# A two-layer, two-block network on one core: a new order for the first stage (early products of ones, bias rows, memory root, index heads)

## The chip, the cores and the metric

The kernel runs on one core of a Trainium2 chip. The metric is the device time of one execution in microseconds (us), as the median of several executions. A core has TensorE (PE, with its weight loads as PEld), VectorE (DVE), ScalarE (ACT), GpSimd (POOL) and SyncE (SP), which here only issues DMAs. Engines run their own instructions in order and wait for each other by semaphores.

## What is computed

Four layers on x of 256 rows by 1024 columns: two layers of a first network (each a mixer and a convolutional feed-forward part), then two of a second one, whose mixers also attend to a memory of 256 rows. The change lies in the first mixer, and it is enough to see this much of the reference:

```
h = x @ w_in                      # q_a, c_kv, q_idx, k_idx, w_idx, q_b, k_b, v_b, f_in
log_f = log_sigmoid(f_in + b_f); cum_f = cumsum(log_f)
idx = einsum('bthd,bsd->bths', q_idx, k_idx)             # 8 index heads
score = einsum('bth,bths->bts', w_idx, relu(idx)); sel = top_k(score, 64)
la = q_lat . c_kv[sel] + rel_bias[t5_bucket(q_pos - sel)]   # path a: 8 heads over the selected keys
lb = q_b . k_b + cum_f[q] - cum_f[k]                        # path b: 8 heads, causal
mem_n = rmsnorm(mem, mem_norm_g)                            # used by the second network
```

All arithmetic is float32. A product is split: a weight tile `raw` is rounded to a high part `whi`, and the rest is a low part `wlo`; the activations are split the same way, and three products are summed.

## The kernel before

**Weights.** `schedule()` lists all weight tiles in the order of their use: `ev_a` (tiles 0 to 6, `ea` = 0), `ev_v` (7, 8), `ev_b` (9, 10, `eb` = 9), `ev_c` (11), `ev_o` (12 to 15) and so on. A tile is 128 x 2048 and goes through three buffers of each kind: SP loads `raw` (line 273), ACT writes `whi` (line 295), and then either DVE (line 318) or POOL (line 303, in four pieces of 128x512) writes `wlo`. Tiles 0 and 1 have their low part from DVE, tiles 2 to 15 from POOL. SP may load tile m once the low part of tile m - 3 is made; ACT may write `whi` of a tile once the products of the tile three before are done. The helpers `act_weights(m)`, `pool_weights(m)` and `sp_weights(m)` work through the list up to tile m at the place of the engine's program where they stand.

**Products.** `project(m, bank)` makes 32 products with the high part (lines 365 and 366) and 16 with the low part (line 372), one after the other.

**The prelude.** SP loads the identity and x, PE transposes x (line 882), ACT and DVE split it. PE then starts on tile 0 in `project_first` (lines 401 to 407). Meanwhile POOL splits the table of relative biases in three bf16 parts (lines 930 to 942, waiting for six small DMAs), PE multiplies it out to eight bias rows (line 858), DVE copies them out of PSUM (line 907), and SP writes them to HBM (line 961), to be read back skewed. The memory rows are squared and summed by ACT (line 1257), DVE takes the inverse root by 12 small instructions (`newton`, lines 530 to 547) and scales the rows (line 921), PE transposes them (line 870, `mem_pe`), and ACT copies them out (line 901, `mem_act`).

**The order of the work around the change** is written out by hand in one function per engine. On PE: tile 0, bias rows 0 to 5, tile 1, bias rows 6 and 7, `mem_pe`, tile 2, two small transposes (line 1104), all eight index heads two at a time (line 1118), tiles 3 to 6, the value tiles 7 and 8 (lines 437, 448), tile 9, and then a loop over 16 attention heads in which PE makes scores (lines 1171, 1172), DVE the maximum (line 988), ACT the exponential (line 1004), DVE the normalisation (line 1018) and PE the transposes (line 977). In round 0 of that loop PE also runs tile 10, in round 3 tile 11. On ACT the relu of the index heads (line 1268) follows `mem_act`; on DVE the weighted sum of the heads (lines 1339, 1342) is followed by the forget gates: a sum (line 1361), then ACT loads a table and takes abs, exp and log (lines 1273 to 1278), then three DVE instructions (lines 1363 to 1368). After that DVE fills the extra rows of the b scores (lines 1372 to 1383), selects the 64 best keys in 16 rounds (lines 1355, 1357) and makes their mask (lines 1386 to 1390).

## Time and profile before

| | |
|---|---|
| three executions | 1375.17, 1376.55, 1378.96 us |
| median | 1376.55 us |
| the profiled execution: device time, its span | 1374.63 us, 1373.3 us |
| PE, DVE, ACT, POOL busy | 98%, 74%, 57%, 13% of the span |
| DMA | 240.85 MB, mean 175 GB/s |

The rows of this document count time from the start of the profiled span. A busy PE is not PE at its peak: starts of neighbouring products tell the rate. "idle before" names what ended an engine's idle time. The granted clock is TensorE's, 1.00 for 2.4 GHz and 0.50 for 1.2 GHz.

### The profile page before, as it was taken

What the parts mean: (1) busy time and instruction counts of PE and PEld (TensorE: products, weight loads), DVE (VectorE), ACT (ScalarE), POOL (GpSimd) and SP (SyncE); (2) the same over time, 40 slices, a digit from 0 to 9 for tenths busy, and PEclk for the clock granted to TensorE, in tenths of its full rate; (3) what the DMA queues carried; (4) which work ended last, traced back from release to release, by engine and by line L of the source; (5) the groups of instructions that cost most, each with busy time, mean ns of one, the idle gap of its engine ahead of it and who ended that gap; (6) DMA issues with size and microseconds to landing.
All of it is one profiled execution on the core that took longest, in us unless ns stands there. A gap on an engine that the chain in (4) does not pass through costs nothing.

```text
span 1373.3 us, 20772 instructions
## 1 busy us (share of the span) xinstructions
PE 1343.9 (98%) x8207; PEld 1161.9 (85%) x8207; DVE 1020.7 (74%) x1684; ACT 783.0 (57%) x1260; POOL 179.0 (13%) x155
## 2 busy tenths in 40 slices
PE   7999999999999999999999999999999999999998
PEld 7886888888898888887977788888689998888887
DVE  5865588777887787778777577767567998787666
ACT  5654366655442666553667466555456875665553
POOL 4860300000100000000034200000212224000000
PEclk9999999999999999999999999999999999999999
DMA  8622265644563556553533065655344444355551
GB/s 314 227 80 121 86 222 214 231 184 184 192 246 123 192 209 243 184 184 108 205 123 118 31 227 204 223 200 188 144 163 161 148 154 185 133 204 200 188 199 73
DMA packets 37215, 240.85 MB, mean 175 GB/s; under 512 B 4096, under 2 KB 6528, under 8 KB 9728
## 3 DMA queue, kind: packets, MB, share of 16 engines
q1 hardware_dynamic: 37120, 239.54, 47.7%
q8 instruction: 65, 1.06, 0.3%
q14 instruction: 30, 0.25, 0.0%
HBM read 236.89 MB, written 2.64 MB: 174 GB/s over the span
## 4 chain that ended last, share of the span: by engine, by line
PE 88%; DVE 6%; ACT 2%; issue 2%; DMA 1%; POOL 1%; SPq 0%; DVEq 0%; ACTq 0%; POOLq 0%
PE ps L385 23%; PE ps L437 16%; PE ps L390 12%; PE ps L448 8%; PE ps L365 5%; PE ps L372 5%; PE ps L366 5%; PE ps L609 2%; PE ps L604 2%; PE ps L977 1%; DVE wlo L318 1%; PE ps L1924 1%; PE ps L580 1%; ACT whi L295 1%; PE ps L2232 1%
## 5 line engine op out<-in xcount | busy, mean ns | idle before, releaser
L318 DVE TENSOR_TENSOR wlo<-raw,whi 128x2048 fp32r<-128x2048 f32 (+1 forms) x178 | 399.6, 2250 | 106.7 <-ACT whi L295 104.7
L295 ACT ACTIVATE whi<-raw 128x2048 fp32r<-128x2048 f32 x203 | 385.8, 1904 | 83.1 <-PE ps L448 40.1
L385 PE MATMUL ps<-XS,whi 128*128 128x512 f32 x1392 | 331.8, 390 | 0.0
L385 PEld LDWEIGHTS ps<-XS,whi 128*128 128x128 f32 x1392 | 257.8, 188 | 52.3 <-issue 0.8
L437 PE MATMUL ps<-whi,MS 128*128 128x512 f32 x960 | 233.6, 391 | 0.0
L437 PEld LDWEIGHTS ps<-whi,MS 128*128 128x128 f32 x960 | 177.5, 188 | 35.9 <-issue 0.4
L303 POOL TENSOR_TENSOR wlo<-raw,whi 128x512 fp32r<-128x512 f32 x114 | 155.4, 1396 | 281.6 <-ACT whi L295 193.4
L390 PEld LDWEIGHTS ps<-XS,wlo 128*128 128x128 f32 x1392 | 178.5, 191 | 6.8
L390 PE MATMUL ps<-XS,wlo 128*128 128x256 f32 x1392 | 180.6, 283 | 0.0
L365 PE MATMUL ps<-XS,whi 128*128 128x256 f32 x672 | 166.8, 288 | 0.0
L366 PE MATMUL ps<-XS,whi 128*128 128x256 f32 x672 | 162.9, 283 | 0.0
L1517 ACT ACTIVATE ar<-ps 128x256 f32<-128x256 f32 x176 | 57.3, 377 | 146.6 <-PE ps L390 146.4
L524 POOL TENSOR_TENSOR st<-st 128x1 f32<-128x1 f32 x24 | 16.7, 695 | 879.8 <-DVE st L517 879.8
L365 PEld LDWEIGHTS ps<-XS,whi 128*128 128x128 f32 x672 | 128.5, 191 | 1.4 <-issue 0.6
L366 PEld LDWEIGHTS ps<-XS,whi 128*128 128x128 f32 x672 | 128.7, 191 | 0.6 <-issue 0.2
L448 PE MATMUL ps<-wlo,MS 128*128 128x512 f32 x480 | 122.5, 389 | 0.0
L448 PEld LDWEIGHTS ps<-wlo,MS 128*128 128x128 f32 x480 | 90.1, 188 | 18.8
L1543 DVE TENSOR_TENSOR ar<-ps,ar 128x256 f32<-128x256 f32 x176 | 66.1, 418 | 43.4 <-ACT ar L1517 43.4
L372 PE MATMUL ps<-XS,wlo 128*128 128x256 f32 x672 | 88.3, 283 | 0.0
L372 PEld LDWEIGHTS ps<-XS,wlo 128*128 128x128 f32 x672 | 84.0, 192 | 0.0
L1523 ACT ACTIVATE ar<-ar,pc 128x256 f32<-128x256 f32 x88 | 40.0, 502 | 46.9 <-DVE ar L1543 46.9
L505 ACT ACTIVATE MS<-ar 128x256 fp32r<-128x256 f32 x104 | 42.1, 405 | 22.7 <-DVE ar L1572 9.6
(327 smaller groups left out, 1537.2 us busy)
## 6 DMA issues: line engine op xcount, KB each, us to landing
raw<-in_up SPq DMA_DIRECT2D x88, 1024.0 KB, 4.8
raw<-in_down SPq DMA_DIRECT2D x44, 1024.0 KB, 4.9
raw<-in_hg_t SPq DMA_DIRECT2D x16, 1024.0 KB, 4.8
raw<-in_od_t SPq DMA_DIRECT2D x8, 1024.0 KB, 5.2
raw<-in_ev_a SPq DMA_DIRECT2D x6, 1024.0 KB, 9.3
raw<-in_wa_o SPq DMA_DIRECT2D x6, 1024.0 KB, 5.0
raw<-in_hg_o SPq DMA_DIRECT2D x6, 1024.0 KB, 4.8
raw<-in_ev_o SPq DMA_DIRECT2D x4, 1024.0 KB, 5.8
```

Source lines behind the costliest of these rows:

```text
L295: ac.activation(parts_of(m)[0][:, 0:w], raw[m % NRAW][:, 0:w], ACT.Copy).then_inc(w_hi)
L303: ins = po.tensor_tensor(lo[:, c], r[:, c], hi[:, c].bitcast(F32), ALU.subtract)
L318: ve.tensor_tensor(lo[:, c], r[:, c], hi[:, c].bitcast(F32), ALU.subtract).then_inc(w_lo_v)
L365: pe.matmul(d, hi[:, c], XS[:, k, 0:256], start=(k == 0 and i == some[0]), stop=False)
L366: pe.matmul(d, hi[:, c], XS[:, k, 256:512], start=False, stop=False)
L372: last = pe.matmul(d, lo[:, c], XS[:, k, 0:256], start=False, stop=(k == 7 and i == some[-1]))
L385: pe.matmul(banks[i][:, 0:512], hi[:, c], XS[:, k, 0:512], start=(k == 0), stop=False)
L390: last = pe.matmul(banks[i][:, 0:256], lo[:, c], XS[:, k, 0:256], start=False, stop=(k == 7))
L437: pe.matmul(accs[tt][h][:, 0:c], x, hi[:, n * j + c * h:n * j + c * h + c], start=(begin and x is sh), stop=False)
L448: ins = pe.matmul(accs[tt][h][:, 0:c], sh, lo[:, n * j + c * h:n * j + c * h + c], start=False, stop=end)
L1517: ac.activation(o[:, 256 * i:256 * i + 256], b[:, 256:512], ACT.Copy).then_inc(f_cb.up())
L1543: ins = ve.tensor_tensor(o[:, c], up_banks(k, j)[i][:, 0:256], o[:, c], ALU.add)
```

## The change

- PE makes eight products of ones, 128x512 in bf16, before it waits for x. The ones are written by DVE (`busy`), the result is not used.
- The six small DMAs of the bias table and the one-hot rows become two, of the same bytes.
- SP issues tile 3 ahead of the mask and constants, and tile 5 ahead of the wait for the bias rows.
- PE runs tiles 0 and 1, then bias rows 0 to 5, tile 2 (after the fifth copy), bias rows 6 and 7, the two small transposes, `mem_pe`, tile 3, index heads 0 to 3, tile 4, index heads 4 to 7, tile 5.
- The root of the memory rows is one scaling on DVE and one power on POOL for each half (`root_dve`, `root_pool`, lines 514 to 524). DVE waits for the squares ahead of the copies of the bias rows; POOL makes the powers behind the low part of tile 2.
- ACT makes `mem_act` after the second copy of the index queries and ahead of `whi` of tile 5. It makes the relu of heads 4 to 7 after the gates' logarithm.
- DVE makes the forget gates between index heads 3 and 4.
- Tile 10 is run as one 128x256 block in round 0 and one in round 1. ACT makes `whi` of tiles 12 and 13 behind the exponentials of rounds 0 and 3 and not ahead of them.

```diff
         def prelude_pe():
+            pe.wait_ge(busy.sem, 1)
+            for _ in range(8):
+                pe.matmul(bank[0][:, :], idle[:, 0:128], idle, start=True, stop=True)
             pe.wait_ge(d_id, 16)
...
         def prelude_dve():
             ve.memset(mhalf, -0.5).then_inc(half.up())
+            ve.memset(idle, 1.0).then_inc(busy.up())
...
             dve_weights(1)
+            ve.wait_ge(m_sq.sem, 2)
+            for tt in range(2):
+                root_dve(st[:, 22 + tt:23 + tt], st[:, 20 + tt:21 + tt], 1.0 / 1024, RMS_EPS)
             bias_rows_dve(range(6))
-            ve.wait_ge(m_sq.sem, 2)
-            newton(st[:, 22:24], st[:, 20:22], 1.0 / 1024, RMS_EPS)
+            root_ready()
...
         def prelude_pool():
-            po.wait_ge(d_oh, 96)
+            po.wait_ge(d_oh, 32)
...
+            pool_weights(2)
+            for tt in range(2):
+                root_pool(st[:, 22 + tt:23 + tt])
...
         def prelude_sp():
-            for i in range(3):
-                sp.dma_start(onehot[32 * i:32 * i + 32], T["c_onehot"]).then_inc(d_oh, 16)
-                sp.dma_start(rel[32 * i:32 * i + 32], T["c_par"][0:32, a:b]).then_inc(d_oh, 16)
+            sp.dma_start(onehot, bass.AP(tensor=hot.tensor, offset=hot.offset, ap=[[0, 3], [384, 32], [1, 384]])).then_inc(d_oh, 16)
+            sp.dma_start(rel, bass.AP(tensor=par.tensor, offset=par.offset + PC["relb"][0],
+                                      ap=[[0, 3], [NPC, 32], [1, 8]])).then_inc(d_oh, 16)
             sp_weights(2)
             for i in range(2):
                 sp.dma_start(gb[:, i, :], T["mem_2"][0, 128 * i:128 * i + 128]).then_inc(d_mem[i], 16)
+            sp_weights(3)
             sp.dma_start(mask, T["c_mask"]).then_inc(d_cb, 16)
             sp.dma_start(cc[:, 128:], T["c_f32"][:, 128:]).then_inc(d_cc, 16)
-            sp_weights(4)
+            sp_weights(5)
             sp.wait_ge(b_out.sem, 8)
...
         def even_pe():
             project_first(bank[4])
+            project(ea + 1, bank[5])
             pe.wait_ge(r_pt.sem, 8)
             bias_rows_pe(range(6))
-            project(ea + 1, bank[5])
+            pe.wait_ge(b_out.sem, 5)
+            project(ea + 2, bank[6])
             bias_rows_pe((6, 7))
-            mem_pe()
             pe.wait_ge(b_out.sem, 6)
-            project(ea + 2, bank[6])
             pe.wait_ge(e_ac.sem, 1)
...
-            for h in range(0, 8, 2):
...
+            mem_pe()
+            pe.wait_ge(e_ac.sem, 2)
             project(ea + 3, bank[4])
+            index_heads(range(0, 4))
             project(ea + 4, bank[5])
+            index_heads(range(4, 8))
             project(ea + 5, bank[6])
...
-                if i == 0:
+                if i in (0, 1):
                     pe.wait_ge(e_ac.sem, 12)
-                    project(eb + 1, bank[7])
+                    project(eb + 1, bank[7], blocks=(i,))
...
+        def index_heads(heads):
+            for h in heads:
+                if h < 4:
+                    pe.wait_ge(e_ac.sem, 3)
+                    pe.wait_ge(m_ev.sem, 8)
+                else:
+                    pe.wait_ge(e_ac.sem, 4)
+                    pe.wait_ge(e_re.sem, h - 3)
...
+                for tt in range(2):
...
+                    ins = pe.matmul(bank[h % 4][:, a:b], QI[q, c:c + 128], KI[q, 0:b - a], start=True, stop=True)
+                ins.then_inc(e_ix.up())
...
         def even_act():
...
             for j in range(2):
                 act_weights(ea + 3 + j)
-                if j:
-                    mem_act()
...
+            mem_act()
             act_weights(ea + 5)
+            index_act(range(0, 4))
             z = slice(0, 104)
             ac.wait_ge(e_fz.sem, 1)
...
             heads_of(ea + 3, 1, QX, 0, 0.125)
+            index_act(range(4, 8))
...
                     soft_act(i, 0, eS, eP, eNM, esegs)
+                if i == 0:
+                    act_weights(eb + 3)
+                if i == 3:
+                    act_weights(ec + 2)
```

On DVE the eight instructions and waits of the forget gates move, unchanged, between `index_dve(range(0, 4))` and `index_dve(range(4, 8))`, the two halves of the former loop over heads.

## Rows read from the trace of the kernel before

**Rows 1.** The page: busy time, share of the span and instructions of each engine.

```profile
PE 1343.9 (98%) x8207; PEld 1161.9 (85%) x8207; DVE 1020.7 (74%) x1684; ACT 783.0 (57%) x1260; POOL 179.0 (13%) x155
```

**Rows 2.** Stretches: length, busy time per engine, granted clock, DMA share, GB/s.

```profile
10.00:14.80 4.80, 4.75 (x23) 4.78 (x24) 3.03 (x4) 3.29 (x3) 0.00 (x0) 1.00 1.05 340
...
34.90:40.75 5.85, 3.48 (x35) 2.32 (x34) 4.44 (x11) 3.06 (x7) 3.38 (x3) 1.00 1.01 402
...
94.00:137.00 43.00, 40.42 (x248) 29.09 (x246) 27.04 (x90) 18.73 (x73) 4.56 (x4) 1.00 0.25 98
```

**Rows 3.** PE's waits, 0 to 137 us: total, times, longest.

```profile
PE ps L1118 <- ACT ar L1268: 2.4, 2, 2.0
```

**Rows 4.** Groups of PE instructions, 0 to 20 us, shapes apart: busy, mean ns.

```profile
L404 PE MATMUL ps<-XS,whi 128*128 128x256 f32 x8 | 1.9, 415 | 0.0
...
L372 PE MATMUL ps<-XS,wlo 128*128 128x256 f32 x8 | 1.1, 282 | 0.0
```

**Rows 5.** Timeline of DVE, 18.7 to 28.5 us: start, length, instruction.

```profile
19.14 2.88 DVE L907 COPY ar<-ps 128x384 f32<-128x384 f32 x6 [2.60 <-PE ps L858]
21.94 0.64 DVE L530 TENSOR_SCALAR nw<-st 128x2 f32<-128x2 f32 x1
22.61 1.21 DVE L532 TENSOR_SCALAR st<-nw 128x2 int32<-128x2 int32 x1
```

**Rows 6.** Timeline of POOL, 13 to 110 us.

```profile
18.76 5.03 POOL L303 TENSOR_TENSOR wlo<-raw,whi 128x512 fp32r<-128x512 f32 x4
...
56.06 25.48 POOL L303 TENSOR_TENSOR wlo<-raw,whi 128x512 fp32r<-128x512 f32 x18 [0.57 <-ACT whi L295]
```

**Rows 7.** The root elsewhere: DVE's scaling (min/median/max ns), POOL's power (mean ns).

```profile
L517 DVE TENSOR_SCALAR st<-st x24: 153/154/155, 156.6 to 1369.0; 128x1 f32<-128x1 f32 x24
...
L524 POOL TENSOR_TENSOR st<-st 128x1 f32<-128x1 f32 x24 | 16.7, 695 | 879.8 <-DVE st L517 879.8
```

**Rows 8.** Timeline of ACT, 13 to 110 us.

```profile
21.10 0.20 ACT L1257 ACTIVATION_READ_ACCUMULATOR yb<-gb 128x1 f32 x1
...
30.38 3.01 ACT L901 ACTIVATE ar<-ps,pc 128x256 f32<-128x256 f32 x8
...
44.23 1.28 ACT L1273 ACT_TABLE_LOAD   x1
...
81.73 1.91 ACT L295 ACTIVATE whi<-raw 128x2048 fp32r<-128x2048 f32 x1
```

**Rows 9.** The chain that ended last, 0 to 160 us: start, length, what.

```profile
44.77 1.92 PE ps L372 x16
50.53 1.92 PE ps L372 x16
```

**Rows 10.** Timeline of DVE, 28 to 60 us.

```profile
36.50 1.94 DVE L1339 TENSOR_SCALAR ar<-ar 128x128 f32<-128x128 f32 x2 [1.26 <-ACT ar L1268]
38.36 4.83 DVE L1342 SCALAR_TENSOR_TENSOR ar<-ar 128x128 f32<-128x128 f32 x14
...
43.78 0.35 DVE L1361 TENSOR_SCALAR ar<-ar,pc 104x256 f32<-104x256 f32 x1
...
50.39 0.91 DVE L1372 MEMSET ar<- 64x1024 f32 x1 [0.27 <-DVE ar L1368]
```

**Rows 11.** Timeline of DVE, 60 to 110 us.

```profile
79.03 2.73 DVE L1386 TENSOR_SCALAR ar<-ar 128x384 f32<-128x384 f32 x1
...
82.34 0.61 DVE L988 TENSOR_REDUCE ar<-ps 128x1 f32<-128x128 f32 x2
```

**Rows 12.** The chain that ended last, 76 to 99 us.

```profile
88.77 0.92 ACT ar L1004 x4
89.74 0.49 PE ps L1171 x2
```

**Rows 13.** Stretches behind a PE wait later in the kernel, columns as in rows 2.

```profile
711.00:714.20 3.20, 0.74 (x8) 0.55 (x7) 2.47 (x5) 3.20 (x7) 0.66 (x1) 1.00 1.01 366
714.40:717.60 3.20, 2.99 (x11) 2.27 (x10) 3.10 (x5) 1.53 (x5) 3.20 (x3) 0.50 0.45 179
```

More of the change, by code:

```diff
@@ L244, in program @@
         cb_in = mark("cb_in")
-        half = mark("half")
+        half, busy = mark("half"), mark("busy")
         nv, nr, ly, tp = mark("nv"), mark("nr"), mark("ly"), mark("tp")
@@ L850, in program @@
         r_pt = mark("r_pt")
+        idle = gp[:, 0:256].bitcast(BF16)
         x_bank = [[6, 7], [2, 3]]
@@ L1234, in posts_a, with index_act @@
                           stop=True).then_inc(e_po.up())
+        def index_act(heads):
+            for h in heads:
+                ac.wait_ge(e_ix.sem, h + 1)
+                if h >= 2:
+                    ac.wait_ge(e_sc.sem, 2 * h - 2)
+                ac.activation(RR[h % 2], bank[h % 4][:, 0:384], ACT.Relu).then_inc(e_re.up())
         def even_act():
```

71 lines of the change are left out of this document (28 added, 43 removed).

## The prediction

> **What bounds the kernel now.** I read the page's shares first, then PE by stretches, PE's waits, and the engines' timelines of the first 100 us. PE is busy for 98% of the span [rows 1], and from the attention loop on nearly always (40.4 of 43.0 us up to 137 us) [rows 2]. So what PE gains ahead of the loop stays gained, and nothing behind it is touched. Before the loop PE loses time in three ways. It runs at the lower clock until about 14.8 us: the same 128x256 products show 415 ns there and 282 ns later [rows 4]. The view of the granted clock gives 1.00 even in that stretch [rows 2], so here the lengths of the products decide, and they are those of 1.2 GHz. It waits 2.4 us at the index heads [rows 3], where it is busy for 3.5 of 5.85 us [rows 2]. And it waits for the memory rows and their root. The edits aim at all three. The question is what stands behind them.
>
> **The key reading** is how DVE and POOL meet. Beside POOL's pieces of low part (18.76 to 23.79 us, four pieces of 1.26 us [rows 6]) a DVE scaling of two elements took 0.64 us and one more 1.21 us [rows 5]. Their ends, 22.58 and 23.82, are the ends of the third and the fourth piece. With POOL idle a scaling of one element took 0.15 us in all 24 cases [rows 7]. PSUM copies are not held up: six in 2.88 us, one each 0.47 us [rows 5], under the same pieces. So a small DVE scaling out of SBUF waits for the end of the running POOL piece. The Trainium skill says the same (SBUF — State Buffer, section "SBUF: two separate sides"): a DVE instruction in a two-port mode, or with two SBUF inputs, and a GpSimd instruction exclude each other for the whole instruction. It speaks against the new place of the root: that rule gives 2.4 us for the two scalings, and by free scalings they would be 0.3 us.
>
> **The change, step by step**, on the time axis of the profiled execution.
>
> 1. Ones, two DMAs in place of six, blocks 0 and 1. If the ones bring the clock up before tile 0, its 24 cold products (4.8 us, rows 2) take 2.9 at 0.12 us each, and the transposes end about 0.9 us sooner. Tiles 0 and 1 then end near 20.7 us (14.85 + 5.8; a tile is 48 products and takes 50.53 - 44.77 = 5.76 us [rows 9]). With the clock as before they end at 23.6. The ones themselves lie in PE's idle time before x, so they cost nothing there; the DMAs save only issue time of SP, whose transfers queue at a full DMA share of 1.00 and more [rows 2]. Six bias rows add 1 us to PE: 21.7, or 24.6.
> 2. The root. DVE must wait for the squares, which end at 21.30 as before [rows 8], since the memory rows land no sooner. The two scalings then meet the same two POOL pieces as lines 530 and 532 and end at 22.6 and 23.82. Price between 0.3 us (free, rows 7) and 2.5 us; I take 2.5, because the two-element rows are the nearest in place and partner [rows 5]. The nine other instructions of the old root vanish. POOL's powers (0.7 us each, rows 7) start at 23.8 and end by 25.2, under DVE's copies. Tile 3's low part starts only then, still 3 us before it did.
> 3. Bias copies. The fifth ends at 23.85 + 4 x 0.47 + 0.55 = 26.3 us, and PE waits for it before tile 2. PE therefore starts tile 2 at 26.3 in place of 28.8, whichever clock it had: 2.5 us sooner, and the ones are worth nothing here, since PE only waits longer.
> 4. PE to the index heads: tile 2 5.9, two bias rows 0.3, small transposes 0.2, memory transposes 1.9, tile 3 5.85: 40.5 us. ACT's eight copies (3.0 us, rows 8) and `whi` of tile 5 are hidden by tile 3. If tile 3 were shorter than 5 us the heads would wait for them. The first head is with DVE 1.25 us later, at 41.75; before it was 36.50 [rows 10]. So PE's wait of 2.4 us is gone, but DVE begins its own chain 5.25 us later.
> 5. DVE chain. The opening pair of scalings again meets POOL (now on tile 5) and I keep 1.94 us; six more additions at 0.345 make 2.05: 45.75. Gates: 0.35, table load 1.28, abs 0.4, exp and log 0.9, then subtraction 0.3 and scan 0.55 free of POOL, since tile 6's `whi` now comes behind the relus: 49.6. Behind the logarithm ACT evicts tile 3 (1.1 us) before relu 4, so head 4 starts at 50.25. Four heads take 2.75 us and the two masks 0.5: 53.5. The memsets stood at 50.39 [rows 10], so here the chain is 3.2 us late: 2.0 of the 5.25 come back from fewer meetings with POOL and from the gates' waits.
> 6. From the memsets to the first maximum the instructions are the same, 31.95 us before (50.39 to 82.34 [rows 10, 11]). In it line 1386 sat 2.73 us until POOL's long run ended at 81.54 [rows 6, 11]. POOL's run for tile 6 now starts at 54.1, and its last piece (tile 11) ends at 83.9, while DVE comes to line 1386 at 82.25. It loses 1.75 us, not 2.73. The first maximum comes at 84.75: 2.4 us late.
> 7. The loop. Exponential 0 from 85.4 to 86.3, then `whi` of tile 12, moved behind it, 1.91 [rows 8]: 88.2. Exponential 1 then ends at 89.1, and PE's third-round scores start at 89.15; before 88.77 + 0.92 and 89.74 [rows 12]. PE itself is there at 86.7: its lead of 2.5 us and the split tile 10 buy only this. **Sum: 0.6 us faster.** Tile 13's move saves under 0.5 us in round 3 or nothing; I count nothing.
>
> The profiled execution took 1374.63 us, 1.9 below the median of 1376.55; the sum as a difference applies to the median: 1376.0 us.
>
> **Rivals.**
> (B) *Free roots and a warm start.* If one-element scalings pass POOL's pieces, and the ones have raised the clock, the fifth copy ends at 24.15, and everything from step 3 on comes 2.15 us sooner: 2.7 faster, 1373.8. For it: all 24 scalings of 0.15 us; against it: POOL was idle in all of them [rows 7].
> (C) *The clock falls in the new wait, slower than before.* With an early clock PE is done with the bias rows at 21.7 and idles until 26.3, 4.6 us. Later in this kernel the granted clock was 0.50 for 3.2 us right behind an idle stretch of 2.5 us (0.74 of 3.2 us busy) [rows 13]. Half speed for 3.2 us costs tile 2 1.6 us, and all of it is on DVE's chain: 1.0 slower, 1377.6. It decides if the wait before tile 2 is at least as long as that idle stretch; the 2.4 us of case B are near it too. The Trainium skill (TensorE: Matmul & The Clock Gate, section "Why this matters for your kernels") also warns of idle gaps between bursts of products; and it holds (section "Part 4: PE-mode transpose") that transposes don't count as work for the clock, by which the ones might be undone before tile 0. That would change nothing in my sum, where the clock is worth nothing.
> (T) *Another table load.* Relu now runs behind the load for exp and log. If that table does not serve it, ACT loads twice more, ahead of relu 4 and ahead of exponential 0, 2 x 1.28 [rows 8] on the chain: 2.0 slower, 1378.6. Copies and exponentials run behind the load today without another one, which speaks against it.
> (D) *POOL does not hold DVE at all in the new places.* Roots 2.15, the opening pair 1.3, line 1386 1.75 less: 5.8 faster, 1370.7. All three at once are unlikely, two of them give about 4.
> The change does what it says in every case; only the ones may not raise the clock, and that is the main sum's case already.
>
> **Numbers.** Forecast 0.42, B 0.20, D or most of it 0.16, C 0.12, T or T with C 0.10. A measurement of this kernel tells 0.3%, 4.1 us, from no change. Forecast, B, C and T alone stay inside. Faster by more needs D: 0.18 with B and a part of it. Slower by more needs C and T together and one further meeting of DVE with POOL at heads 4 to 7: 0.06. The rest, 0.76, is no difference. The range goes from two thirds of D (5.1 faster, 1371.5) to C with T less a little (1379.5).
>
> **What would show it.** Right: tile 2 (products behind line 372's first groups) starts at 26.3; the roots' scalings last 1.2 us each; no PE wait at the index heads; the first index scaling at 41.8; the first maximum at 84 to 85.5; the third scores within 1 us of 89.7; from there a constant shift. Wrong in step 2 if the scalings show 0.15 us and tile 2 starts near 24; wrong in step 1 if tile 0's products are still 415 ns; a granted clock of 0.50 between 24 and 30 us is C; table loads near 50 and 85 us are T; a first maximum before 82.3 us refutes the bound by DVE's chain.

## The result, and the profile after

The changed kernel takes **1381.32 us** (median of seven, 1380.02 to 1385.87) beside 1375.50 us for the kernel before in the same comparison: a ratio of **1.0043, 95% interval 1.0033 to 1.0052**, 5.9 us slower. The forecast was 1376.0 us, no difference, with a range that ended at 1379.5 us. The profiled execution is the slowest of the seven (1385.87 us, span 1384.5 us), so its own sum has to account for 11.2 us of span, of which some 4.5 us are peculiar to it. The two profiled executions are the two ends in the clock as well: their mean granted clock is 0.999 before and 0.991 after, while the other six executions of the changed kernel show 0.994 to 0.996, and those of the kernel before that were timed beside the experiments 0.996 to 0.997 in the mean.

The page, first part, answers to [rows 1]. PE is busy for 8.4 us more than before. 3.6 us of that are the eight products of ones, which lie ahead of x, where PE was idle before; the other 4.8 us are the same products taking longer, and the 6.4 us that are then left of the 11.2 are waiting:

```profile
PE 1352.3 (98%) x8215; PEld 1166.6 (84%) x8215; DVE 1022.3 (74%) x1675; ACT 783.1 (57%) x1260; POOL 179.7 (13%) x157
```

**Ahead of tile 2.** SyncE's timeline (start, length, what it issues). The two merged DMAs cost 2.1 us to issue, and the load of tile 2 behind them held the queue for 4.19 us; before, the six small DMAs took 2.8 us and that load 0.49 us:

```profile
4.19 0.89 SPq L961 DMA_DIRECT2D ar<-in_c_onehot  x1
5.13 1.21 SPq L962 DMA_DIRECT2D ar<-in_c_par  x1
6.38 4.19 SPq L273 DMA_DIRECT2D raw<-in_ev_a  x1
10.62 0.90 SPq L966 DMA_DIRECT2D gb<-in_mem  x2
```

So POOL's bias table starts at 17.62 us and not at 15.03, `whi` of tile 2 at 19.86 and not at 16.77, and, ACT working in order, the squares of the memory rows end at 24.40 and not at 21.30 [rows 8]. ACT's timeline:

```profile
19.86 1.92 ACT L295 ACTIVATE whi<-raw 128x2048 fp32r<-128x2048 f32 x1 [4.69 <-DMA raw<-in_ev_a]
24.20 0.20 ACT L1279 ACTIVATION_READ_ACCUMULATOR yb<-gb 128x1 f32 x1
```

DVE's timeline, to be held against [rows 5, 10, 11]. The root's two scalings took 0.21 us together, although POOL was in the middle of four pieces (next fence). The first scaling of the index heads came at 45.32 us, 8.8 us later than before; the mask (line 1409) again stood for 2.7 us:

```profile
24.43 0.21 DVE L517 TENSOR_SCALAR st<-st 128x1 f32<-128x1 f32 x2 [6.93 <-ACT yb L1279]
24.56 2.87 DVE L911 COPY ar<-ps 128x384 f32<-128x384 f32 x6
...
45.32 1.63 DVE L1351 TENSOR_SCALAR ar<-ar 128x128 f32<-128x128 f32 x2 [4.81 <-ACT ar L1256]
...
57.00 0.91 DVE L1395 MEMSET ar<- 64x1024 f32 x1 [0.27 <-DVE ar L1379]
...
62.15 1.74 DVE L1405 COPY gb<-cc 8x1024 f32<-8x1024 f32 x1
...
86.65 2.69 DVE L1409 TENSOR_SCALAR ar<-ar 128x384 f32<-128x384 f32 x1
...
89.92 1.14 DVE L999 TENSOR_REDUCE ar<-ps 128x1 f32<-128x128 f32 x4
```

POOL's timeline, to be held against [rows 6]. One run of 22 pieces ends at 89.12 us, and tiles 12 and 13 follow inside the attention loop:

```profile
21.86 4.94 POOL L303 TENSOR_TENSOR wlo<-raw,whi 128x512 fp32r<-128x512 f32 x4 [1.92 <-ACT whi L295]
26.77 1.07 POOL L524 TENSOR_TENSOR st<-st 128x1 f32<-128x1 f32 x2
...
57.22 31.90 POOL L303 TENSOR_TENSOR wlo<-raw,whi 128x512 fp32r<-128x512 f32 x22 [10.42 <-ACT whi L295]
93.36 5.03 POOL L303 TENSOR_TENSOR wlo<-raw,whi 128x512 fp32r<-128x512 f32 x4 [4.24 <-ACT whi L295]
99.82 4.99 POOL L303 TENSOR_TENSOR wlo<-raw,whi 128x512 fp32r<-128x512 f32 x4 [1.43 <-ACT whi L295]
```

PE's waits up to 145 us (total, times, longest). The first is the wait for the fifth bias copy, the second the wait for the normalisations in the loop; the third row is the latter in the kernel before:

```profile
PE ps L365 <- DVE ar L911: 4.4, 1, 4.4
PE ps L988 <- DVE ar L1029: 3.3, 3, 2.1
```

```profile
PE ps L977 <- DVE ar L1018: 1.6, 2, 1.3
```

Stretches (columns as in [rows 2]): PE idle, then tile 2 at a granted clock of 0.50, then its rest at 1.00; a stretch inside the attention loop at 0.50, where PE was busy throughout; and the place near 720 us that [rows 13] showed before:

```profile
22.60:26.20 3.60, 0.03 (x1) 0.00 (x0) 1.77 (x6) 3.10 (x5) 3.60 (x4) 0.99 0.97 399
26.30:33.00 6.70, 5.99 (x28) 5.99 (x29) 4.58 (x5) 2.90 (x3) 6.70 (x7) 0.50 0.50 189
33.10:35.60 2.50, 2.50 (x23) 2.44 (x22) 0.00 (x0) 0.00 (x0) 2.50 (x3) 1.00 0.00 0
...
104.70:108.10 3.40, 3.40 (x16) 2.28 (x13) 2.05 (x9) 1.57 (x6) 0.11 (x1) 0.50 0.00 0
...
722.50:729.20 6.70, 6.28 (x19) 5.06 (x19) 5.67 (x11) 3.75 (x12) 4.41 (x4) 0.50 0.37 125
```

**The chain in the loop** (start, length, what): two normalisations that take 0.55 us with POOL idle took 2.4 us beside the pieces of tiles 12 and 13, with PE's transposes (line 988) right behind them.

```profile
93.63 2.38 DVE ar L1029 x2
96.06 0.55 PE ps L988 x3
...
101.28 2.41 DVE ar L1029 x2
103.74 0.55 PE ps L988 x3
```

The milestones of the two profiled executions, and the lead or lag (us):

| | forecast | before | after | after - before |
|---|---|---|---|---|
| squares end | 21.3 | 21.3 | 24.4 | 3.1 |
| fifth bias copy | 26.3 | 21.6 | 27.0 | 5.4 |
| first index scaling | 41.75 | 36.5 | 45.3 | 8.8 |
| memsets (line 1395, 1372) | 53.5 | 50.4 | 57.0 | 6.6 |
| first maximum | 84.75 | 82.3 | 89.9 | 7.6 |
| third-round scores | 89.15 | 89.7 | 94.1 | 4.4 |
| first output product (line 437) | as above | 137.2 | 145.0 | 7.8 |
| span | | 1373.3 | 1384.5 | 11.2 |

Behind the first output product the last 3.4 us are clock: 0.50 for 6.8 us at 722.5 us where before it was 3.4 us, and for 3.4 us at 1193.5 us where before there was no such stretch; 6.8 us more at half speed lose 3.4 us. These stretches come and go between kernels that run the same instructions there, so I count them as no part of the change. That is not quite shown: the long one near 720 us stands in six of the nine profiled kernels with the new loop part, and in one of the eleven without it.

**How much of this is one execution.** a_loop and a_pool, two of the kernels below, run the changed kernel's instructions up to the first index scaling. It came at 42.70 and 42.66 us in their profiles, 2.6 us sooner than in the table and 0.9 us behind the forecast. b_loop and b_pool run those of the kernel before, and show 36.48 and 38.66. So the 8.8 us of the table lie between a late execution and an early one; the forecast's 5.25 us are well inside what the others show (4.0 to 6.2). Of the clock there is an estimate for the timed executions: one less the mean granted clock, times the span, is 7.7 us for the seven of the changed kernel and 4.5 to 5.6 us for those of the kernel before, so up to 2 or 3 of the 5.9 us are clock (less, as far as it fell while PE had nothing to do).

### The profile page after: what moved, and what is told of

Read it like the earlier page. It is cut to its first block, busy times and chain, and to the rows that moved or that the text cites. A ratio compares the mean times of both kernels' runs of the same rounds, so it can differ in the third digit from the quotient of the medians.

```text
span 1384.5 us, 20785 instructions
## 1 busy us (share of the span) xinstructions
PE 1352.3 (98%) x8215; PEld 1166.6 (84%) x8215; DVE 1022.3 (74%) x1675; ACT 783.1 (57%) x1260; POOL 179.7 (13%) x157
## 4 chain that ended last, share of the span: by engine, by line
PE 86%; DVE 6%; ACT 3%; POOL 2%; issue 2%; DMA 1%; SPq 0%; DVEq 0%; ACTq 0%
PE ps L385 23%; PE ps L437 15%; PE ps L390 12%; PE ps L448 8%; PE ps L365 5%; PE ps L366 5%; PE ps L372 5%; PE ps L609 2%; PE ps L604 2%; POOL wlo L303 1%; PE ps L988 1%; DMA raw<-in_ev_a 1%; PE ps L1947 1%; DVE wlo L318 1%; ACT whi L295 1%
## 5 line engine op out<-in xcount | busy, mean ns | idle before, releaser
L365 PE MATMUL ps<-XS,whi 128*128 128x256 f32 x672 | 169.5, 292 | 4.4 <-DVE ar L911 4.4
L366 PE MATMUL ps<-XS,whi 128*128 128x256 f32 x672 | 165.3, 285 | 0.0
L448 PEld LDWEIGHTS ps<-wlo,MS 128*128 128x128 f32 x480 | 90.1, 188 | 18.7
## 6 DMA issues: line engine op xcount, KB each, us to landing
raw<-in_ev_a SPq DMA_DIRECT2D x6, 1024.0 KB, 11.2
```

The source lines that it names most:

```text
L365: pe.matmul(d, hi[:, c], XS[:, k, 0:256], start=(k == 0 and i == some[0]), stop=False)
L366: pe.matmul(d, hi[:, c], XS[:, k, 256:512], start=False, stop=False)
L448: ins = pe.matmul(accs[tt][h][:, 0:c], sh, lo[:, n * j + c * h:n * j + c * h + c], start=False, stop=end)
```

## The experiments

The expectations name theories by letters. **W**: the loss is made ahead of tile 2 (merged DMAs, late squares, a wait in which the clock falls). **S**: the index heads, split and put behind tile 3, start DVE's chain too late, and that chain decides when the loop can run. **G**: POOL's pieces hold the mask's scaling. **P**: POOL's pieces for tiles 12 and 13 hold the normalisations in the loop. **K**: speed ahead of the memory rows is worth nothing. Where an expectation says it otherwise, its own words hold. All ratios are to the kernel before, timed beside it on the same chip; its median was 1376.08 us in the first set, 1376.74, 1375.65 and 1376.50 us in the next three, and 1376.20 us for a_pool and b_best. A ratio compares all executions and not the medians, and the two can differ: most for a_noidx, whose medians give 1.0039. Two ratios of different sets are told apart only as far as both intervals allow.

**First set, theory W.** Three kernels are the changed one with one thing undone or added, the fourth is the kernel before with one thing of the change.

```diff
 a_dma6     # after, with the six DMAs of before
-            po.wait_ge(d_oh, 32)
+            po.wait_ge(d_oh, 96)
 a_noones   # after, without the eight products of ones
 a_fill     # after, with products of ones in the wait for the fifth copy
             bias_rows_pe(range(6))
+            pe.wait_ge(e_ac.sem, 2)
+            for _ in range(20):
+                pe.matmul(bank[4][:, :], idle[:, 0:128], idle, start=True, stop=True)
 b_dma2     # before, with the two merged DMAs
```

> The changed kernel with the six small DMAs of the bias table in place of the two merged ones. Theory W (the loss is made ahead of tile 2: late memory rows, then the wait for the fifth bias copy with the fall of the clock in it): tile 2's raw data lands near 16.8 us and not 19.2, the squares end near 21.3, the fifth copy near 24.3, PE idles under 2 us there and the clock stays at 1.00, tile 2 ends near 30.2 in place of 35.5, and the execution is 4 to 5.5 us faster than the changed kernel, 1376 to 1377.5. Rival L (the loss is made in the vector chain and in the attention loop, where POOL's pieces hold DVE): the early stretch shifts as said, but less than 1.5 us of it is left at the end.

> The changed kernel without the eight products of ones. Theory W: the clock comes up near 14 us, tile 1 ends near 24.5, PE idles under 2 us for the fifth copy, the clock does not fall at 26 us, tile 2 runs in 5.8 us and ends near 33.1, and the execution is about 2.4 us faster than the changed kernel: the ones do harm here. Rival L: no difference beyond 1 us. Rival O (the ones are a gain of 1 to 3 us that something else hides): slower by that.

> The changed kernel with 20 more products of ones in PE's wait for the fifth bias copy (4.3 us of work at the high clock, in a wait of 4.4). Theory W: nothing moves before 27 us, but the clock stays at 1.00, tile 2 runs in 5.8 us in place of 8.5, and 2.7 us are gained at the end. Rival L: the early gain is there, less than 1 us of it at the end.

> The kernel before with only the six small DMAs merged into two. Theory W: tile 2's raw data lands 2.4 to 3 us later, near 19.3, SP is held for about 4 us at the issue behind the merged DMAs, the bias rows come 2 us later; the memory rows' scaling ends 2 to 3 us later, so tile 2 starts that much later and the execution is 1.5 to 3 us slower than before. Rival M (the merged DMAs cost nothing that isn't hidden): within 0.7 us of before.

| | median, us | ratio, 95% interval |
|---|---|---|
| a_dma6 | 1381.69 | 1.0046, 1.0029 to 1.0064 |
| a_noones | 1382.18 | 1.0046, 1.0034 to 1.0058 |
| a_fill | 1380.35 | 1.0035, 1.0021 to 1.0048 |
| b_dma2 | 1376.25 | 1.0002, 0.9994 to 1.001 |

W falls as the main cause. With the products in the wait the clock stays up and tile 2 takes its 6 us again, and yet the kernel is still 4.8 us slower than before. a_noones is no faster than the changed kernel, and b_dma2, which W put 1.5 to 3 us behind the kernel before, can't be told from it. These are the stretches of a_fill, its wait filled and tile 2 behind it:

```profile
22.00:25.40 3.40, 3.34 (x17) 1.57 (x16) 2.52 (x8) 2.90 (x4) 3.40 (x4) 1.00 1.01 419
25.40:32.20 6.80, 6.80 (x55) 6.29 (x53) 3.95 (x4) 2.26 (x2) 6.80 (x6) 1.00 0.58 222
```

What W named is in the traces, though in part smaller than W had it. With two DMAs in the kernel before SyncE again holds the next load for 3.90 us and the squares end 1.9 us late, at 23.18 us. With six DMAs in the changed kernel the squares end at 22.65 us, but the fifth copy still at 26.4 us, where W said 24.3: there the granted clock fell at 10.6 us, PE made the bias rows 2.1 us later than in the changed kernel, and the copies waited for them. None of this is where the time is decided.

**Second set, theories S and G.** b_idx also has the gates between the heads on DVE and relu 4 to 7 behind them on ACT; a_loop also has `whi` of tiles 12 and 13 back ahead of exponentials 0 and 3.

```diff
 b_idx      # before, with the index part alone
             project(ea + 3, bank[4])
+            index_heads(range(0, 4))
             project(ea + 4, bank[5])
+            index_heads(range(4, 8))
...
 a_loop     # after, with its loop part undone
-                if i in (0, 1):
-                    project(eb + 1, bank[7], blocks=(i,))
+                if i == 0:
+                    project(eb + 1, bank[7])
...
 b_loop     # before, with that loop part alone
 a_mix      # after, with six DMAs, the filled wait, and the loop part undone
```

> The kernel before with one part alone: tile 3, index heads 0 to 3, tile 4, heads 4 to 7, tile 5 on PE, the relus of heads 4 to 7 behind the gates' logarithm on ACT, the gates between heads 3 and 4 on DVE. Theory S (the split is what costs: it puts DVE's chain behind tile 3, and DVE's chain sets the start of the attention loop): first index scaling near 42 in place of 36.5, QX memset near 53.9 in place of 50.4, first maximum near 86.5 in place of 82.3; the loop's output products start 1 to 4 us later than before and the execution is 2 to 4 us slower than before. Rival N (the heads' place is neutral, since PE gains its 2.4 us of waiting): within 1 us of before or faster.

> The changed kernel with the loop part undone: tile 10 whole in round 0, high parts of tiles 12 and 13 ahead of the exponentials. Theory P (POOL's low parts of tiles 12 and 13, made later, hold DVE's normalisations in rounds 3 to 6 and PE waits 2 us for them): third scores up to 2 us later than in the changed kernel, but the stretch from the third scores to the output products shrinks by 1.5 us or more, plus 1.7 if the clock no longer falls near 104 us; in sum 0 to 3 us faster than the changed kernel. Rival Q (the loop part is a gain): 1 to 2 us slower than the changed kernel.

> The kernel before with the loop part alone: tile 10 in two blocks, high parts of tiles 12 and 13 behind the exponentials of rounds 0 and 3. Theory P: the third scores come up to 2 us sooner, but the normalisations meet POOL, so that at most 1 us is left at the output products, or up to 1.5 us is lost. Rival Q: 1 to 3 us faster than before.

> The changed kernel with the six small DMAs, with 20 products of ones in the wait for the fifth copy, and with the loop part undone. If the loss is the sum of the DMAs (1 us), the clock in the wait (2.7 us), and the loop part (theory P, 1.5 us or more), this comes within 1.5 us of the kernel before. If the split of the index heads costs 3 us or more by itself (theory S), it stays 2 to 4 us slower than before.

| | median, us | ratio, 95% interval |
|---|---|---|
| b_idx | 1383.26 | 1.0053, 1.0033 to 1.0072 |
| a_loop | 1381.47 | 1.0038, 1.0022 to 1.0054 |
| b_loop | 1377.82 | 1.0014, 1.0003 to 1.0025 |
| a_mix | 1385.44 | 1.0063, 1.0047 to 1.0079 |

S holds for the kernel before: the index part alone costs 7.3 us (0.0053 x 1376.7; by the interval 4.5 to 9.9 us, by the medians 6.5), about as much as the whole change or more. The first index scaling of its profiled execution came at 46.9 us, where 42 was expected. And G shows itself in its sharpest form. The timelines of b_idx, POOL and then DVE: POOL runs 26 pieces without a gap, to 95.06 us, and the mask's scaling, started at 87.64, ends 0.2 us behind them:

```profile
58.21 36.85 POOL L303 TENSOR_TENSOR wlo<-raw,whi 128x512 fp32r<-128x512 f32 x26 [10.93 <-ACT whi L295]
```

```profile
87.64 7.64 DVE L1398 TENSOR_SCALAR ar<-ar 128x384 f32<-128x384 f32 x1
```

At some 1.4 us a piece that is more than five pieces, not the rest of one. PE then waits 4.5 us for the exponential. a_mix, which was to be the cheap version, met the same run of pieces (its scaling took 7.65 us) and is the slowest kernel of the study, 8.7 us slower than before, where 1.5 us or 2 to 4 us had been expected: undoing the loop part puts `whi` of tile 12 ahead of exponential 0 again, and POOL goes from tile 11 to tile 12 without a gap.

A run without a gap is not enough for it, though. a_loop has the same 26 pieces, and DVE got in after each of its instructions was held for a while; from the mask's scaling to the first maximum it took 5.2 us, beside 8.2 in b_idx and 3.3 in the kernel before. a_loop's timelines, POOL and then DVE:

```profile
54.59 37.08 POOL L303 TENSOR_TENSOR wlo<-raw,whi 128x512 fp32r<-128x512 f32 x26 [10.41 <-ACT whi L295]
```

```profile
84.03 1.45 DVE L1409 TENSOR_SCALAR ar<-ar 128x384 f32<-128x384 f32 x1
85.52 1.20 DVE L1411 TENSOR_SCALAR ar<-ar 128x128 bf16<-128x128 f32 x1
86.63 2.69 DVE L1413 SCALAR_TENSOR_TENSOR ar<-ar,cb 128x128 bf16<-128x128 f32 x2
```

So undoing the loop part in the changed kernel frees the loop (47.8 us from the third scores to the first output product and not 50.9, PE's wait for the normalisations 1.7 us and not 3.3) and makes the mask dearer. The timed difference of 0.7 us between a_loop and the changed kernel (1.0038 and 1.0043) is well within the intervals.

**Third set: an early split.** Heads 0 to 3 stay where they were, ahead of tile 3, and only heads 4 to 7 go behind it.

```diff
 b_early, b_early_loop   # before, and before with the loop part
+            index_heads(range(0, 4))
             project(ea + 3, bank[4])
+            index_heads(range(4, 8))
             project(ea + 4, bank[5])
 a_noidx                 # after, with its index part undone
 b_idx_loop              # before, with index part and loop part
```

> The changed kernel with the index part undone: all eight heads ahead of tile 3, relus and gates in the old order. Theory S (the split of heads puts DVE's chain behind tile 3): the first index scaling comes 3 to 4 us sooner than in the changed kernel (near 41 in place of 45), PE waits 2 to 4 us at the heads, the loop's third scores come 1 to 4 us sooner, and the execution is 2 to 4 us faster than the changed kernel. Rival N (the split is neutral): within 1 us of the changed kernel.

> The kernel before with the index part and the loop part. Theory G (in the run with the index part alone the mask's scaling of 128x384 waited 7.64 us, through six pieces of POOL's low parts that ran back to back into tile 12; it gets POOL's shared access only when POOL's run has a gap): with tile 12's high part behind the first exponential POOL has nothing to go on with, the scaling waits under 3 us, the first maximum comes about 5 us sooner than with the index part alone, and the execution is 2 to 5 us faster than with the index part alone, but still 1 to 4 us slower than before. Rival H (the long wait is chance): the scaling's wait is not tied to tile 12's place.

> The kernel before with heads 0 to 3, tile 3, heads 4 to 7, tile 4 on PE, gates between the heads on DVE. Theory S: the first index scaling stays near 36.5, PE's wait of 2.4 us at the heads goes, tile 6 ends near 62 in place of 64. By theory G this can backfire: PE's lead brings tile 12's high part ahead of the end of POOL's run, and the mask's scaling then waits over 7 us; then the first maximum comes near 87 and the execution is 1 to 4 us slower than before; without that 1 to 3 us faster.

> The same with the loop part (tile 12's high part behind the first exponential). Theory G: the mask's scaling waits under 3 us, the first maximum comes between 81 and 84, PE's lead of 2 us reaches the loop; the loop part costs 1 to 1.5 us by itself, so the execution is between 1 us faster and 1 us slower than before, and 2 to 5 us faster than the run without the loop part, if that run shows the wait over 7 us.

| | median, us | ratio, 95% interval | mask scaling, us |
|---|---|---|---|
| a_noidx | 1381.08 | 1.0030, 1.0018 to 1.0042 | 1.50 |
| b_idx_loop | 1382.55 | 1.0050, 1.0037 to 1.0063 | 1.46 |
| b_early | 1377.95 | 1.0013, 1.0000 to 1.0025 | 7.69 |
| b_early_loop | 1377.68 | 1.0012, 1.0004 to 1.0021 | 2.70 |

The scaling took 1.46 us in b_idx_loop beside a run of pieces that went on to 88.27 us, so it isn't always held to the end; there the next instruction was. DVE's timeline of b_idx_loop:

```profile
85.69 1.46 DVE L1398 TENSOR_SCALAR ar<-ar 128x384 f32<-128x384 f32 x1
87.19 1.18 DVE L1400 TENSOR_SCALAR ar<-ar 128x128 bf16<-128x128 f32 x1
```

b_early against b_idx (0.0013 against 0.0053, 5.5 us, by the intervals some 2 to 9) is the price of having the index heads one tile later, 0 to 3 behind tile 3 and 4 to 7 behind tile 4: both have the gates between the heads, and both have the mask's wait of 7.6 us.

Two expectations of this set failed. The loop part was to win back 2 to 5 us where the mask waits over 7 us; the wait went (7.64 to 1.46, 7.69 to 2.70) and the time did not (1.0053 to 1.0050, 1.0013 to 1.0012). And undoing the index part in the changed kernel was to win 2 to 4 us; a_noidx is 1.8 us faster by the ratios (1.0043 to 1.0030), and their intervals overlap. There the index part costs much less than the 7.3 us that it costs alone.

**Fourth and fifth set, theory P, and what is left ahead of tile 3.** Only the place of POOL's pieces is changed, by two waits:

```diff
 b_pool, b_early_pool, a_pool
         def even_pool():
+            pool_weights(ec)
+            po.wait_ge(e_mb.sem, 3)    # tile 12: behind the mask
+            pool_weights(eo)
+            po.wait_ge(a_nm.sem, 8)    # tile 13: behind the eighth maximum of path a
 b_ones   # before, with the eight products of ones alone
 a_pre    # after, with index part and loop part undone
 b_best   # b_early_pool with the eight products of ones
```

> Before, with two waits added on POOL: the low part of tile 12 starts only after the mask of the selected keys is made, that of tile 13 only after the eighth maximum of path a. Theory P (POOL's pieces in the loop hold DVE's normalisations and through them PE): the wait of PE on the normalisation (1.6 us in three waits before) falls to 0.5 us or less, the third scores to the first output product shrink from 47.5 us to 46 or less, the time falls by 0.5 to 1.5 us: 1374.5 to 1375.5. Rival (the pieces only move and meet other DVE work): no change within 0.5 us, or slower by up to 1 us when the pieces of tile 12 meet the maxima. The mask scaling stays at 2.7 us in both, as it waits for tiles 9 to 11 there.

> Before, with index heads 0 to 3 ahead of tile 3, heads 4 to 7 behind it, the gates between them, and the two POOL waits of the run above. Theory P with G (the mask scaling is starved by pieces in a row): the scaling takes under 2.7 us in place of 7.69 us of the same kernel without the POOL waits, the first maximum comes near 83 us in place of 88.3, the third scores at 86.5 to 88 in place of 91.6, the first output product at 134.5 to 136.5 in place of 139.9; the time is 1372.5 to 1375, the first version under before. Rival (PE fills the gap anyway, what is won at the loop's start is waited for inside it): 1375.5 to 1377.

> Before with the eight products of ones alone. Theory K (PE's speed before the memory rows is worth nothing, since PE waits for them): tiles 0 and 1 end 2.5 to 3 us sooner, PE then waits 4 to 5.5 us ahead of the transposes of the memory rows in place of 2.1 to 2.9, tile 2 starts as before, time within 0.3 us of before; if the granted clock falls behind that wait, as it did in the changed kernel, 0.5 to 2.5 us slower. Rival (a warm start is worth what it saves): 1 to 2.5 us faster, tile 2 starts sooner.

> The changed kernel with both its index part and its loop part undone: what is left is ones, two DMAs, the order of the bias rows and of tiles 0 to 2, the root and the places of tiles 3 and 5. The index part alone cost 7.0 us, the loop part alone 1.9, all together 5.5. Theory S (the loss is the index split and what it triggers): this kernel is within 1.5 us of before, 1375 to 1377. Rival W (the part ahead of tile 3 is itself a loss: a longer wait for the fifth copy, a fall of the clock behind it, squares 3.1 us later): 1378 to 1380, as the version without the index part (1381.1, with the loop part worth 1.5 of it) hints.

> The changed kernel with the two waits on POOL (tile 12's low part behind the mask, tile 13's behind the eighth maximum of path a). Theory P: the stretch from the third scores to the first output product, 50.9 us in the changed kernel and 47.5 before, falls to about 48 and the PE wait on the normalisation from 3.3 to about 1 us; the time falls by 1.5 to 3 us, to 1378 to 1380, still slower than before, since the first index scaling stays behind tile 3. Rival (POOL is only half of it, the late start of DVE's chain leaves PE waiting however POOL stands): 1380.5 to 1382.

> Before with heads 0 to 3 ahead of tile 3, heads 4 to 7 behind it, gates between them, the two POOL waits and the eight products of ones. If the gains add up (2.3 us for the early split with the POOL waits, 1.1 us for the ones, the latter no more than the interval): 1373 to 1374. Rival (the ones are worth nothing, as PE waits for the memory rows anyway): as without them, 1374.2, and if the clock falls behind the wait, 1375 to 1376.

| | median, us | ratio, 95% interval |
|---|---|---|
| b_pool | 1375.31 | 0.9990, 0.9981 to 0.9999 |
| b_early_pool | 1374.17 | 0.9983, 0.9974 to 0.9992 |
| b_ones | 1375.61 | 0.9992, 0.9983 to 1.0 |
| a_pre | 1376.65 | 1.0006, 0.9997 to 1.0015 |
| a_pool | 1379.07 | 1.0016, 1.0008 to 1.0025 |
| b_best | 1373.83 | 0.9982, 0.9973 to 0.9991 |

P holds. The same two waits take 3.7 us from the changed kernel (1.0043 to 1.0016), 4.1 us from b_early (1.0013 to 0.9983), each give or take some 2 us by the intervals, and 1.4 us from the kernel before, whose interval nearly reaches 1. They answer G as well as P, since the first wait keeps tile 12 away from the mask and the second tile 13 from the normalisations; they were not timed apart. In a_pool the stretch from the third scores to the first output product is 49.7 us (50.9 in the changed kernel, 47.5 before). The forecast was 48; the granted clock was 0.50 for 3.4 us at 93.7 us there, which costs up to 1.7. In b_pool it shrank to 47.1 us and not to 46, and PE's wait fell from 1.6 us to 1.0 and not to 0.5. PE's waits up to 140 us of b_loop, b_pool and a_pool, in that order, show the same wait with the pieces of tiles 12 and 13 beside the first normalisations, and moved away:

```profile
PE ps L977 <- DVE ar L1018: 3.7, 3, 2.1
```

```profile
PE ps L977 <- DVE ar L1018: 1.0, 3, 0.4
```

```profile
PE ps L988 <- DVE ar L1029: 1.9, 4, 0.9
```

b_early_pool's timelines, POOL and then DVE, show an early split once POOL leaves the room: the mask is done at 85.2 us (in b_early its scaling alone ended at 87.7), and the normalisations are at 0.55 us:

```profile
52.34 32.03 POOL L303 TENSOR_TENSOR wlo<-raw,whi 128x512 fp32r<-128x512 f32 x22 [4.31 <-ACT whi L295]
85.33 4.98 POOL L303 TENSOR_TENSOR wlo<-raw,whi 128x512 fp32r<-128x512 f32 x4 [0.96 <-DVE ar L1402]
108.68 4.94 POOL L303 TENSOR_TENSOR wlo<-raw,whi 128x512 fp32r<-128x512 f32 x4 [18.36 <-DVE ar L1018]
```

```profile
81.82 2.77 DVE L1398 TENSOR_SCALAR ar<-ar 128x384 f32<-128x384 f32 x1
...
91.89 0.55 DVE L1018 TENSOR_SCALAR ar<-ar 128x128 f32<-128x128 f32 x2
```

My numbers for it were only partly right: the scaling took 2.77 us and not less than 2.7, the first maximum came at 85.2 us and not near 83, the third scores at 90.0 us and not at 86.5 to 88, but its first heads had themselves started 2.6 us later than in the kernel before (39.1 and 36.5), so this profile understates it; the timed gain, 2.3 us, is inside what was expected. How much of it is the split is open: b_pool, with the two waits alone, was timed beside it at 0.9990, and the intervals overlap.

a_pre settles W: everything ahead of tile 3 together costs 0.8 us, within the interval of nothing.

With it, all eight combinations of the three parts have been timed (ratios to the kernel before):

| | neither | loop part | index part | both |
|---|---|---|---|---|
| without the part ahead of tile 3 | 1 | 1.0014 (b_loop) | 1.0053 (b_idx) | 1.0050 (b_idx_loop) |
| with it | 1.0006 (a_pre) | 1.0030 (a_noidx) | 1.0038 (a_loop) | 1.0043 (the change) |

Each part is in four of the eight. The mean of its four differences is 0.0034 for the index part (4.6 us), 0.0010 for the loop part (1.4 us) and 0.0000 for the part ahead of tile 3, each give or take 0.0009 by the intervals. Together that is 6.0 us, and the change costs 5.9.

In b_ones the stretches show why the ones are worth so little where they stand. 2.0 us into a wait of 3.5 us for the bias table PE's clock falls, and the next 6.7 us are granted 0.50:

```profile
15.40:17.40 2.00, 0.00 (x0) 0.00 (x0) 1.16 (x1) 0.72 (x1) 1.77 (x4) 0.99 0.99 399
17.40:24.10 6.70, 5.31 (x22) 4.47 (x23) 4.66 (x10) 3.81 (x7) 6.00 (x9) 0.50 1.03 416
```

Tile 1 ended at 28.1 us, later than before (25.7), and the first index scaling came 1.2 us later, but the memsets stood at 50.43 us (50.39 before) and the first output product at 137.23 (137.20). The time was 1.1 us shorter, or the same by the end of its interval. That a fall of the clock there costs 0.5 to 2.5 us, as I expected, is refuted for this kernel. b_best is the fastest kernel of the study, 2.5 us faster than before, but it can't be told from b_early_pool.

## Why the prediction was wrong

**Held.** Step 1: with the ones the first products take about 0.29 us in place of 0.415 us. Tile 1 ends at 21.6 us, 0.9 us later than forecast: the transposes were done sooner, but tile 0 then waited 2.5 us for its `whi` (line 288) and began at 9.86 us, hardly sooner than before (10.05). Nor is the warm start certain: in four of the ten profiled kernels with the ones the granted clock fell near 10 or 11 us for 3.4 us. The chain from the first index scaling to the memsets is 11.7 us (45.32 to 57.00); step 5 gave 11.75. PE's wait at the index heads is gone. No further table load came (rival T): the one load near 49 us served relu and exponentials as well.

**Step 2 failed twice, and the errors nearly cancelled.** It priced the two scalings at 2.5 us by the two-element rows; they took 0.21 us under POOL's pieces. Rival B's condition was met: a reading of two-element rows was carried over to one-element rows. But step 2 also said that the squares end "at 21.30 as before, since the memory rows land no sooner", and step 1 gave the merged DMAs as a saving. They end 3.1 us later, behind the load of tile 2, which held the queue for 4.19 us behind the merged DMAs. Over all profiled kernels the squares end at 22.8 to 24.4 us in the eight with merged DMAs (next load held for 3.2 to 4.3 us) and at 20.8 to 22.7 us in the twelve with six (0.4 to 0.6 us). Rival B's gain of 2.15 us was spent before it came. The merged DMAs read three copies of the same rows, with the copies as their outermost step. The Trainium skill (DMA: Bandwidth & Descriptors, section "Rules for kernel authors") says that such a broadcast of c copies confines a DMA to at most c engines. That agrees with the long hold; that only three engines worked is not shown by any row here.

**Step 3 and rival C.** The wait before tile 2 was 4.4 us (I had 4.6), and the clock fell, for 6.8 us and not for 3.2. Tile 2 took 8.6 us in place of 5.9. So case C, which I gave 0.12, was the one that came, with 2.7 us and not 1.6. Together with 0.7 us on the fifth copy this is 3.4 of the 3.6 us by which the first index scaling missed its forecast in this execution. In a_loop and a_pool the fifth copy ended at 25.4 us, the clock fell for 3.4 us, and the miss was 0.9 us. So steps 3 and 4 were about right for the kernel and wrong for this execution; without the fall (a_fill) the time is 1.1 us shorter by the ratios (1.0043 and 1.0035), which the intervals don't tell from nothing.

**Step 6** said that the instructions from the memsets to the first maximum are the same and take 31.95 us less one us. They took 32.9 us, and 32.6 to 33.0 us in the five other profiled kernels with this index part and loop part. The constants' copy (line 1405 now, 1382 before) took 1.74 us where its like of before took 0.68 us, since POOL's run of pieces now begins ahead of both copies and not between them; and the scaling of the mask lost 2.69 us, not 1.75. The latter is an error of the working: POOL's run, from 54.1 us, holds 22 pieces, which at 25.48 / 18 = 1.42 us each [rows 6] end at 85.2 us and not at 83.9. (Its terms also add up to 84.5 us for the first maximum, not to 84.75.)

**Step 7, "from there a constant shift", is the step that cost most.** I counted nothing for the move of `whi` of tiles 12 and 13. It moved POOL's pieces onto the first normalisations, and the loop lost 3.4 us (47.5 to 50.9): 1.7 us of waiting for the normalisations (1.6 to 3.3) and 1.7 us of clock, at 0.50 for 3.4 us from 104.7 us on with PE busy. a_fill runs the same loop without that fall in 49.3 us. The fall goes with the waits: between 90 and 106 us the clock fell in ten of the twelve profiled kernels that have the loop part or the mask's wait of over 7 us, and in none of the eight others. b_loop prices that part alone at 1.9 us timed, with PE's wait at 3.7 us in place of 1.6; a_pool shows that some 3.7 us of the changed kernel's 5.9 go with the place of these pieces. My own key reading, that a POOL piece holds a DVE scaling out of SBUF, was applied in the first 85 us and not in the loop behind them.

**The balance of steps 4 to 7** left too little of the late start. It traded PE's wait of 2.4 us for a start of DVE's chain that lies 5.25 us later, and took 5.8 us back: 2.0 from fewer meetings up to the memsets, 0.8 up to the first maximum, and 3.0 by `whi` of tile 12 behind exponential 0. b_idx shows the trade by itself, without the ones, the DMAs and the loop part: 7.3 us slower; over all combinations it costs 4.6 us. In the changed kernel 8.8 us at the first index scaling are 6.6 at the memsets and 4.4 at the third scores. DVE's chain, not PE, sets when the loop can begin, so a product moved ahead of the first index head is paid for in good part, and filling PE's wait brought no time where it was done by the heads' place alone (b_idx, b_early). Against it, the split one tile sooner (b_early) costs 1.8 us, at the edge of its interval, and with POOL moved the kernel is faster than before.

**The chances.** No difference had 0.76 and a time slower by more than 0.3% had 0.06, which was to need C and T and one more meeting of DVE with POOL. C came, T did not, and the meetings came in the loop.

**The sum** of the profiled execution against the forecast: 3.6 (first index scaling) + 1.4 (from there to the third scores: 1.7 of step 6, and 0.3 back) + 3.4 (loop) + 3.4 (clock behind it) = 11.8 us, which is the 11.2 us more span and the 0.6 us forecast as a gain. The median execution lost 5.9 us. How much of the median's is the clock near 26 us is open: falls came at 20, 26, 95 and 105 us in some profiled kernels and not in others, and only one execution of each was profiled. The parts timed alone don't add up either: a_pre 0.8, index 7.3 and loop 1.9 make 10.0 us where the change costs 5.9; their means over all combinations do (6.0 us). The traces show one reason: with the loop part, `whi` of tile 12 comes later and POOL has a gap behind tile 11, and from the mask's scaling to the first maximum DVE takes 3.0 us in b_idx_loop and 8.2 in b_idx; yet timed, b_idx_loop (1.0050) and b_idx (1.0053) are the same. In the profiles the loop gives back 3.9 of these 5.2 us (52.5 us from the third scores to the first output product, and 48.6).

## What to carry to other kernels

Before a wait on one engine is filled with work from ahead, find the chain that sets the next stage's start: here it was VectorE's, 45 us long, and a start 8.8 us later was still 4.4 us at the third scores, while TensorE's wait of 2.4 us, once filled, gave nothing that was measured. When a ScalarE step is moved, follow what it releases: `whi` of a tile releases four GpSimd pieces of some 1.3 us, and moving these was worth 1.4 to 4.1 us. A wait on TensorE can cost twice, since the granted clock fell behind such waits and the work after it ran at half speed for 3.4 us or more. A profile of the slowest execution says in part what that execution met: compare kernels that share their instructions up to a milestone before a cause is named. A long run of GpSimd pieces should be broken, by a wait, just ahead of a VectorE instruction out of SBUF that others wait for.

## What the runs showed of the hardware that I had not expected

- **A DVE scaling can be held through a whole run of POOL pieces**, not only to the end of the one that runs: 7.64 us in b_idx, 7.69 us in b_early, 7.65 us in a_mix, each ending 0.2 us behind the last piece; in other kernels it got in after 1.5 us, in a_loop beside the same run of 26 pieces. The Trainium skill (SBUF — State Buffer, section "SBUF: two separate sides") speaks of a lock for one instruction and of whoever starts first; by that rule it would have waited for one piece, at most some 1.4 us. The runs don't show what decides between the two; a gap in POOL's run doesn't, as a_loop shows.
- **One-element scalings passed POOL's pieces**: two in 0.21 us at 24.43 us, with POOL busy from 21.86 to 26.80. All nine profiled kernels with this root show 0.14 to 0.15 us for each. The Trainium skill (VectorE: DVE Perf Modes, section "What auto-detection actually checks") gives a one-source instruction the two-port mode if source and destination are in SBUF and their outermost non-unit dimensions are both even or equal. A single element has no such dimension; that it therefore stays out of that mode would explain it, but is only argued.
- **Fewer DMAs were dearer**: two merged ones held the next load for 4.19 us (3.90 in b_dma2), where it had taken 0.49 us behind six.
- **The clock can fall for 6.8 us** (the change: 26.2 to 33.0 us) 3.6 us after PE had run out of work, and 2.0 us after (b_ones); a_loop and a_pool, with the same instructions, have 3.4 us in place of the former. A wait that is filled with products of no use (a_fill) kept it at 1.00.
